# Attention's opening row maxima inside the recurrence's last steps

## The chip, the core and the metric

One NeuronCore of one Trainium2 chip runs the whole kernel in one launch. The metric is the device time of one execution in microseconds (us); less is better. The core has five engines, each with its own queue of instructions that it works through in order: PE multiplies matrices (PEld loads its weights), DVE, ACT and POOL work on vectors, and SP issues DMAs. They meet only through semaphores and, between stages, a barrier of all engines.

## The reference, cut to what matters

One decoder layer on 4096 tokens of width 1024. A projection gives the columns of three mixers; their outputs are gated, multiplied by `W_out`, normalised and added to `x`.

```python
def fox_attention(...):                        # 8 heads of 64, causal
    qh = rms_norm(heads(q), q_gain) * HEAD_DIM ** -0.5
    kh = rms_norm(heads(k), k_gain)
    cum = cumsum(log_sigmoid(f_logit + f_bias))
    s = qh @ kh.T + cum[t] - cum[s]            # s <= t
    o = softmax(s) @ vh
def rwkv7_time_mix(...):                       # 4 heads, a recurrence over all tokens
    sa = state @ -kk_t
    state = state * w_t + sa * (kk_t * a_t) + v_t * k_t
    o_t = state @ r_t                          # then group norm, gain, bias, bonus
y = concat([y_fox, y_rwkv, y_pool]) * silu(g)
x = x + gate * rms_norm(y @ w_out, norm_post)
```

## The kernel before

Five stages run one after the other, each with its own semaphores and buffers and a barrier behind it: set-up, projection (up to about 1397 us), `recur` (up to 1979.7), `attend` (up to about 3190) and `output`.

**`recur`.** The tokens are cut into 16 blocks of 256. A written-out loop, `STEPS = range(-4, BLOCKS + 1)`, runs over steps n = -4 to 16, and in step n every engine works on several blocks at once: block n+3 is prepared (gates, decays, operands), block n+2 gets its scores and its diagonal blocks inverted, block n+1 its triangular inverse, block n goes through the serial chain, block n-1 through the group norm. In steps 13 to 16 the outer blocks are gone, so what is left is the serial chain of blocks 14 and 15 and their norms. The chain of a block has two halves (chunk 0 and 1). On PE it is `right_side` (L1912, L1915), `solve` (L1923), `output` (L1943 to L1949) and `state` (L1933); between them ACT copies the results out of PSUM (`r1_out` L1719, `u_out` L1723), and DVE makes the next state, `state_passed` (L2117). The order of the calls in each engine's part of the loop is the order in its queue. At the end of the chain ACT copies the output (`o_out` L1741) and takes mean and deviation (L1657 to L1673); POOL does `bonus` (L1535, L1538) and `scaled` (L1543 to L1547, four operations on the block's output, `ost`), and SP stores the block (L1426). `negative_mean(b)` on ACT waits for the second operation of `scaled(b - 1)`. Beside all this ACT and DVE split `W_out` into two float16 parts, one row block a step: `w_high` (L1652) and `w_low` (L2135).

**`attend`.** For each of 4 turns of a hardware loop it takes two heads (slots u = 0 and 1). The scores come from two matmuls per unit of 128 keys by up to 512 queries, with the float16 operand pairs `ka`/`qa` and `kb`/`qb` (L2619, L2621). ACT takes the exponential (L2530), POOL or DVE the low part `plo` of the result (L2508, L2721), PE multiplies with `v` (L2600, L2602). The maximum of each row of scores must be known first: for each block of queries PE computes `qa x ka` once more into one of four banks `pm` (L2551 is the causal mask on the diagonal, L2552 the product), DVE takes the largest of each row (L2677). When all maxima of a block of 512 queries are there, POOL adds the decay terms (L2453), DVE takes the largest (L2693, `mp`), POOL splits it into three float16 pieces in seven small operations (L2460 to L2471, into `mw`), PE turns them (L2561) and DVE copies them as three rows of `qb` (L2685). These maxima run `AHEAD` = 49 units ahead of the scores. So before the first turn there is an opening: 49 maxima and 4 rows, 53 items on PE, numbered k = 0 to 52 here. Its operands have to be loaded first (SP, L2376 to L2392), and POOL makes two masks, two identities and constants (L2436 to L2446). Meanwhile DVE and ACT clear the upper rows of `qb` and `kb` (L2651, L2513).

## Time and profile before

| | us |
|---|---|
| runs | 3586.56, 3588.36, 3593.07 (median 3588.36) |
| profiled execution | 3581.05, its span 3579.3 |
| PE busy | 3312.7 (93%) |
| DVE busy | 2415.0 (67%) |
| ACT busy | 1970.1 (55%) |
| POOL busy | 1785.0 (50%) |
| mean granted TensorE clock | 0.96 of full |

The profile's page cuts the span in 40 slices of 89.5 us. PE is 90% busy or more in most of them. Beside the first four, the exceptions are slice 16 (4 tenths), where the recurrence begins, slices 22 and 23 (8 and 6 tenths), where the recurrence ends and attention begins, and slice 36 and the last (7 and 8), around the stage `output`. The rows of the trace that follow further on are from that stretch, from 1906 to 2019 us, but for one on the loop. A row of the timeline gives start, duration, engine, line, operation, the result's and the operands' names with their shapes, how many instructions it stands for, and in brackets how long the engine was idle before it and whom it waited for. PEclk is the granted clock of TensorE as a share of full speed: 1.00 is 2.4 GHz and 0.50 is 1.2 GHz.

### The profile page before, as it was taken

Reading aid. Unit: us, or ns where it says so; the run is one execution under the profiler, and the core shown is the slowest. Engines: PE = TensorE matmul, PEld = TensorE weight load, DVE = VectorE, ACT = ScalarE, POOL = GpSimd, SP = SyncE. Lnnn points to the kernel's source line nnn. Section 1 sums busy time; section 2 is a strip of 40 time slices with the busy share of each in tenths; the row PEclk is TensorE's granted clock in tenths of the full one; section 3 lists DMA queues with packets and bytes.
Section 4 is the critical chain, followed back from the end, with each engine's and each line's share of the span. In section 5 each row is a group of like instructions: output and inputs, shape, how many; then the busy total and the mean of one; then the engine's idle time right before and its main releaser. Section 6 shows DMA issues by size and latency. Waiting matters only on the chain. (4 is left out here: it accounts for less than half of the span.)

```text
span 3579.3 us, 90138 instructions
## 1 busy us (share of the span) xinstructions
PE 3312.7 (93%) x31944; PEld 2298.4 (64%) x31944; DVE 2415.0 (67%) x4337; ACT 1970.1 (55%) x3745; POOL 1785.0 (50%) x2083
## 2 busy tenths in 40 slices
PE   6788999999999994999998699999999999979998
PEld 6783488469549642888888366666666656644444
DVE  5787756326433335786873789899889988965554
ACT  2444544424432234676775477777777777753333
POOL 2376300510330233344553599889988889852222
PEclk9899999999999997898997899999999999989999
DMA  7387445435444533232210312021120220215555
GB/s 313 129 300 254 161 146 169 151 130 178 146 141 155 181 133 89 57 84 69 67 49 28 70 43 59 9 57 36 29 59 10 55 49 17 58 70 181 186 186 180
DMA packets 247770, 401.06 MB, mean 112 GB/s; under 512 B 85646, under 2 KB 199013, under 8 KB 232453
## 3 DMA queue, kind: packets, MB, share of 16 engines
q1 hardware_dynamic: 223979, 383.75, 33.5%
q10 hardware_dynamic: 22880, 11.54, 1.2%
q8 instruction: 258, 4.23, 0.5%
q14 instruction: 173, 1.41, 0.1%
q0 software_dynamic: 480, 0.14, 0.1%
HBM read 272.77 MB, written 122.59 MB: 110 GB/s over the span
## 5 line engine op out<-in xcount | busy, mean ns | idle before, releaser
L2530 ACT ACTIVATE p<-psc,xb,sc 128x512 f32<-128x512 f32 (+3 forms) x1152 | 848.5, 744 | 315.1 <-PE psc L2621 302.1
L2508 POOL TENSOR_TENSOR plo<-p 128x512 f16<-128x512 f32 (+2 forms) x864 | 906.8, 1078 | 66.9 <-ACT p L2530 65.8
L2677 DVE TENSOR_REDUCE mx<-pm 128x1 f32<-128x512 f32 (+3 forms) x1201 | 731.4, 636 | 99.4 <-PE pm L2552 85.8
L646 PE MATMUL bank<-h,ring 128*128 128x512 f16 x2688 | 597.8, 381 | 4.9 <-DVE u L990 4.9
L2600 PE MATMUL po<-v,p 128*128 128x129 f16 x4224 | 513.3, 220 | 20.9 <-POOL plo L2508 18.0
L651 PE MATMUL bank<-ring,h 128*128 128x128 f16 x8064 | 467.0, 222 | 26.7 <-ACT c L818 12.3
L646 PEld LDWEIGHTS bank<-h,ring 128*128 128x128 f16 x2688 | 263.9, 98 | 343.4 <-issue 42.5
L2602 PE MATMUL po<-v,plo 128*128 128x65 f16 x4224 | 483.4, 192 | 0.0
L651 PEld LDWEIGHTS bank<-ring,h 128*128 128x128 f16 x8064 | 463.6, 99 | 28.1 <-issue 12.6
L2600 PEld LDWEIGHTS po<-v,p 128*128 128x128 bf16 x4224 | 388.8, 97 | 121.3 <-POOL plo L2508 28.0
L2602 PEld LDWEIGHTS po<-v,plo 128*128 128x128 f16 x4224 | 379.2, 98 | 96.2
L2552 PE MATMUL pm<-ka,qa 128*128 128x512 f16 (+3 forms) x1201 | 436.8, 367 | 3.1 <-DVE mx L2677 3.0
L1165 POOL CAST stage<-c 128x512 f16<-128x512 f32 x64 | 47.3, 740 | 766.1 <-DVE c L1006 766.1
L2619 PE MATMUL psc<-qa,ka 128*128 128x512 f16 (+3 forms) x1152 | 419.4, 364 | 2.6 <-ACT p L2530 2.4
L2621 PE MATMUL psc<-qb,kb 128*128 128x512 f16 (+3 forms) x1152 | 417.8, 363 | 0.0
L2893 PE MATMUL pz<-wo,yh 128*128 128x512 f16 x1024 | 306.0, 381 | 3.1 <-DVE yl L2925 3.1
L1000 DVE TENSOR_TENSOR c<-bank,u 128x512 f32<-128x512 f32 x168 | 115.6, 689 | 249.6 <-PE bank L646 170.9
L2721 DVE TENSOR_TENSOR plo<-p 128x512 f16<-128x512 f32 (+1 forms) x288 | 280.1, 972 | 0.0
L2837 POOL TENSOR_TENSOR o<-o,xr 128x1024 f32<-128x1024 f32 x32 | 75.4, 2356 | 312.5 <-DVE o L2948 312.5
L2552 PEld LDWEIGHTS pm<-ka,qa 128*128 128x128 f16 x1201 | 118.4, 99 | 134.7 <-DVE mx L2677 15.6
L2893 PE MATMUL pz<-wo,yl 128*128 128x512 f16 x512 | 194.8, 380 | 0.0
L2893 PEld LDWEIGHTS pz<-wo,yh 128*128 128x128 f16 x1024 | 100.5, 98 | 117.8 <-issue 5.2
(417 smaller groups left out, 5583.3 us busy)
## 6 DMA issues: line engine op xcount, KB each, us to landing
ring<-scratch_ws SPq DMA_DIRECT2D x52, 1792.0 KB, 7.8
scratch_z<-stage SPq DMA_DIRECT2D x72, 256.0 KB, 3.2
scratch_ws<-h SPq DMA_DIRECT2D x10, 1792.0 KB, 6.7
y<-scratch_y SPq DMA_DIRECT2D x35, 512.0 KB
g<-scratch_g SPq DMA_DIRECT2D x35, 512.0 KB
xr<-in_x SPq DMA_DIRECT2D x34, 512.0 KB, 6.2
scratch_g<-stage SPq DMA_DIRECT2D x64, 256.0 KB, 6.0
scratch_qk<-stage SPq DMA_DIRECT2D x64, 256.0 KB, 2.6
```

Of the source, the lines that this page charges most:

```text
L646: t = nc.tensor.matmul(bank[b][:], m.ring[:, slot, l, bo, k, :], hh[:, side, r, ao, k, :], start=fresh and first, stop=last, skip_group_ch ...
L651: t = nc.tensor.matmul(bank[b][:, ts], hh[:, side, l, ao, k, ts], m.ring[:, slot, r, bo, k, :], start=fresh and first and tp == 0, stop=la ...
L2508: nc.gpsimd.tensor_tensor(plo[:, k % NP, 0:w], p32[:, k % NP, 0:w], hi[:, 0:w], ALU.subtract)\
L2530: nc.scalar.activation(p32[:, k % NP, 0:w], psc[k % 2][:, 0:w], ACT.Exp, bias=xb[:, u, b, x // 4:x // 4 + 1], scale=m.sc[:, 0:1]).then_inc ...
L2552: ins = nc.tensor.matmul(pm[g][:, n, 0:w], qa[:, u, j * P:(j + 1) * P], ka[:, u, q * BT:q * BT + w], start=not last, stop=True, skip_group ...
L2600: nc.tensor.matmul(o[:, oc:oc + VW], hi[:, c0:c0 + P], v[:, u, x, 0:VW], start=(x == 0 and t % 2 == 0), stop=False, skip_group_check=True)
L2602: g = nc.tensor.matmul(o[:, oc:oc + 1 + HD], plo[:, k % NP, c0:c0 + P], v[:, u, x, 0:1 + HD], start=False, stop=(x == 4 * b + t), skip_gro ...
L2619: nc.tensor.matmul(psc[k % 2][:, 0:w], ka[:, u, ks], qa[:, u, t0:t0 + w], start=not diag, stop=False, skip_group_check=diag)
L2621: nc.tensor.matmul(psc[k % 2][:, 0:w], kb[:, u, ks], qb[:, u, t0:t0 + w], start=False, stop=True, skip_group_check=diag).then_inc(qk_mm.se ...
L2677: nc.vector.tensor_reduce(mx[:, s, t, q:q + 1], pm[g][:, 0, 0:w], AX.X, ALU.max).then_inc(pm_d.sem, 1)
L2721: tt(plo[:, k % NP, 0:w], p32[:, k % NP, 0:w], hi[:, 0:w], ALU.subtract).then_inc(lo_v.sem, 1)
L2893: mm = nc.tensor.matmul(pz[u % 2][j][:], l[:, u % 2, k // 4, ks], r[:, k, j * HALF:(j + 1) * HALF], start=(k == 0 and c == 0), stop=(k == ...
```

## The change

Four things change; the loop of attention itself has the same instructions in the same order as before.

1. **Shared memory.** Some buffers of `recur` (`zf`, `zv`, `sw`, `av`, `ls`, `lc`, `ec`, `ei`, `kk`, `kfac`, `kinv`, `bt`, `kt`, `rk`, `dp`, `onesr`) and slot 0 of attention's operands become pieces of one tensor, `seam`, that lives through both stages. The operands of head 0, the masks, the maxima `mx` and the small rows lie over buffers that the recurrence needs no more after it has prepared block 15.
2. **Operands, masks and clearing move** from attention's start into steps 13 and 14 of the recurrence (`head_operands` and `head_rest` on SP, `head_masks` on POOL, `clear_rows` on DVE). What stays at attention's start is slot 1's: two DMAs, and clearing one half as much on ACT and DVE.
3. **The opening's 53 items move** into steps 15 and 16. On PE they are cut in groups 0 to 7: seven groups of four (k = 0 to 27) between the parts of the serial chain, and the last 25 (k = 28 to 52) behind it. They use two banks in turn, `bank[4 + k % 2]`, where attention had four.
4. `w_high` of the last row block goes behind `inverse_deviation(15)` on ACT.

```diff
+        GROUPS = (4, 4, 4, 4, 4, 4, 4)
# SP
+                    if n == END - 2:
+                        head_operands()
+                    if n == END - 1:
+                        sp.wait_ge(e_clear, 2)
+                        head_rest()
# POOL
+                def head_row(r):
+                    pool.wait_ge(e_done, plan.pre_end[r])
+                    row_sum(nc, m, r).then_inc(e_add, 1)
+                    pool.wait_ge(e_max, r + 1)
+                    for j in range(6):
+                        row_piece(nc, m, j, r % 2).then_inc(e_piece, 1)
+                        pool.wait_ge(e_piece, r * 6 + j + 1)
+                    row_piece(nc, m, 6, r % 2).then_inc(e_row, 1)
                     if there(n - 1):
                         bonus(n - 1)
+                    if n == END - 1:
+                        head_masks()
+                    if n == END:
+                        for r in range(3):
+                            head_row(r)
+                    if n == END + 1:
+                        for r in range(3, plan.EARLY):
+                            head_row(r)
                     ...
                     if there(n - 1):
                         scaled(n - 1)
# ACT
-                    if 0 <= n - 9 < KT:
+                    if 0 <= n - 9 < KT - 1:
                         w_high(n - 9)
                     ...
                         inverse_deviation(n - 1)
+                    if n - 9 == KT - 1:
+                        w_high(n - 9)
# PE, with END = 15; between the lines stand the calls for other blocks
+                def head_maxima(g):
+                    if g == 0:
+                        pe.wait_ge(e_first, 128)
+                        pe.wait_ge(e_made, 1)
+                    for what, item, k in opening[use_at[g]:use_at[g + 1]]:
+                        if k >= 2:
+                            pe.wait_ge(e_done, k - 1)
+                        free = bank[4 + k % 2]
+                        if what == "max":
+                            query_maximum(nc, m, free, m.qa0, m.ka0, item).then_inc(e_mm, 1)
                         right_side(n, 0)
+                        head_maxima(0)
                         solve(n, 0)
+                        head_maxima(1)
                         state(n, 0)
+                        head_maxima(2)
                         right_side(n, 1)
+                        head_maxima(3)
                         solve(n, 1)
+                        head_maxima(4)
                         output(n, 0)
                         state(n, 1)
+                        head_maxima(5)
                         output(n, 1)
+                        head_maxima(6)
+                        head_maxima(7)
# DVE
+                    if n == END:
+                        head_largest(0)
+                        head_largest(1)
                         state_passed(n, 1)
+                    if n == END:
+                        for g in range(2, 6):
+                            head_largest(g)
+                    if n == END + 1:
+                        for g in (6, 7):
+                            head_largest(g)
                     ...
+                    if n == END - 1:
+                        clear_rows()
# attention's start
-                nc.scalar.activation(kb[HD:P, :, :], m.zero[HD:P, :].unsqueeze(2).to_broadcast([HD, 2, SEQ]), ACT.Copy)\
-                    .then_inc(cleared, 1)
+                nc.scalar.activation(kb[1][HD:P, :], m.zero[HD:P, 0:1].to_broadcast([HD, SEQ]), ACT.Copy).then_inc(cleared, 1)
```

`head_largest(g)` on DVE takes the largest of each of the group's banks in turn, and the same small steps for the rows as before. Row 0 is ready for its sum after 4 items, row 1 after 13, row 2 after 26 and row 3 after 43 (`pre_end`).

PE's queue in the middle of step 15, before: `right_side` and `solve` of chunk 0 (`chain_banks<-vt,akr`, `<-Zc,ar`, `<-r,XT`), its `state` (`<-U,bkt`, `<-vt,bkt`), then `right_side` and `solve` of chunk 1.

```order
L1923 MATMUL chain_banks<-r,XT 128x64 x4
L1933 MATMUL chain_banks<-U,bkt 64x64 x2
L1933 MATMUL chain_banks<-vt,bkt 64x64 x2
L1933 MATMUL chain_banks<-U,bkt 64x64 x2
L1933 MATMUL chain_banks<-vt,bkt 64x64 x2
L1912 MATMUL chain_banks<-vt,akr 128x64 x4
L1915 MATMUL chain_banks<-Zc,ar 128x64 x4
L1923 MATMUL chain_banks<-r,XT 128x64 x4
```

PE's queue at the same place of the changed kernel, from the end of that `state` on: L1395 and L1396 are mask and product of a maximum, L2238 the turning of a row, L2179, L2182 and L2190 the chain's `right_side` and `solve`.

```order
L2200 MATMUL chain_banks<-vt,bkt 64x64 x2
L1396 MATMUL bank<-seam 128x512
L1395 MATMUL bank<-seam 128x128
L1396 MATMUL bank<-seam 128x384
L1396 MATMUL bank<-seam 128x512
L2238 MATMUL bank<-seam 128x128 x4
L2179 MATMUL chain_banks<-vt,akr 128x64 x4
L2182 MATMUL chain_banks<-Zc,ar 128x64 x4
L1395 MATMUL bank<-seam 128x128
L1396 MATMUL bank<-seam 128x512 x3
L1395 MATMUL bank<-seam 128x128
L1396 MATMUL bank<-seam 128x128
```

Group 2 now stands between `state` and `right_side`, and group 3 between `right_side` and `solve`, which comes next.

POOL's queue in steps 15 and 16, before: `scaled(14)`, `bonus(15)`, `scaled(15)`.

```order
L1543 TENSOR_TENSOR ost<-ost,st 128x512
L1544 TENSOR_TENSOR ost<-ost,st 128x512
L1545 TENSOR_TENSOR ost<-ost,lng 128x512
L1547 TENSOR_TENSOR ost<-ost,bv 128x512
L1535 TENSOR_TENSOR bv<-vt,bon 128x512
L1538 TENSOR_TENSOR bv<-bv,lnb 128x512
L1543 TENSOR_TENSOR ost<-ost,st 128x512
L1544 TENSOR_TENSOR ost<-ost,st 128x512
```

POOL's queue at the same place of the changed kernel, from the last piece of row 2 on (L1423); L1403 is the sum of row 3, L1412 to L1423 its pieces.

```order
L1423 TENSOR_TENSOR seam<-seam,fixed 128x4
L1772 TENSOR_TENSOR ost<-ost,st 128x512
L1773 TENSOR_TENSOR ost<-ost,st 128x512
L1774 TENSOR_TENSOR ost<-ost,lng 128x512
L1776 TENSOR_TENSOR ost<-ost,bv 128x512
L1764 TENSOR_TENSOR bv<-vt,bon 128x512
L1767 TENSOR_TENSOR bv<-bv,lnb 128x512
L1403 TENSOR_TENSOR seam<-seam 128x4x4
L1412 TENSOR_TENSOR seam<-seam,fixed 128x4
L1414 TENSOR_TENSOR seam<-seam,fixed 128x4
```

Rows 0, 1 and 2 now stand ahead of `scaled(14)`, and row 3 between `bonus(15)` and `scaled(15)`.

## Rows read from the trace of the kernel before

**Rows 1.** Stretches: length, busy time by engine, clock, DMA share, GB/s.

```profile
1947.00:1963.00 16.00, 15.10 (x88) 14.20 (x88) 1.32 (x2) 7.09 (x24) 3.05 (x3) 0.50 0.00 0
1963.00:1979.70 16.70, 0.00 (x0) 0.00 (x0) 1.28 (x1) 7.92 (x30) 8.47 (x8) 0.50 0.09 31
1979.70:1989.30 9.60, 0.00 (x1) 0.03 (x2) 4.18 (x4) 7.03 (x1) 3.46 (x14) 0.50 0.87 186
1989.30:2018.10 28.80, 20.28 (x82) 7.69 (x83) 27.16 (x56) 0.00 (x0) 6.58 (x32) 0.80 0.38 90
```

**Rows 2.** Timeline of PE in step 15 (start, duration, engine, line, operation).

```profile
1942.57 0.66 PE L1915 MATMUL chain_banks<-Zc,ar 64*128 64x64 f32 x8
1943.81 1.07 PE L1923 MATMUL chain_banks<-r,XT 128*128 128x64 f32 x8 [0.57 <-ACT r L1719]
...
1947.18 1.94 PE L1912 MATMUL chain_banks<-vt,akr 128*128 128x64 f32 x8 [0.72 <-DVE Zc L2117]
...
1950.75 1.94 PE L1923 MATMUL chain_banks<-r,XT 128*128 128x64 f32 x8 [0.57 <-ACT r L1719]
1952.48 1.92 PE L1943 MATMUL front<-vt,akr 128*128 128x64 f32 x8
...
1961.74 1.12 PE L1949 MATMUL front<-Zc,ar 64*128 64x64 f32 x8
```

**Rows 3.** Timeline of PE, the opening and the first score.

```profile
1989.30 0.27 PE L2551 MATMUL pm<-mq,idb 128*128 128x128 bf16 x1 [26.44 <-DMA ka<-scratch_nc]
...
2013.02 0.39 PE L2552 MATMUL pm<-ka,qa 128*128 128x512 f16 x1 [0.21 <-DVE mx L2677]
...
2016.96 0.50 PE L2561 MATMUL pm<-id,mw 128*128 128x128 f16 x4 [1.09 <-DVE mx L2677]
...
2018.11 0.31 PE L2617 MATMUL psc<-mk,idb 128*128 128x128 bf16 x1
2018.22 0.63 PE L2619 MATMUL psc<-qa,ka 128*128 128x512 f16 x1
```

**Rows 4.** Timeline of DVE, the next state and the clearing of `qb`.

```profile
1946.56 0.48 DVE L2117 SCALAR_TENSOR_TENSOR Zc<-chain_banks,facs,Zw 128x64 f32<-128x64 f32 x2 [10.25 <-PE chain_banks L1933]
...
1980.62 3.47 DVE L2651 MEMSET qb<- 64x4096 uint32 x1 [11.40 <-PEq L74]
```

**Rows 5.** Timeline of DVE, maxima in a row and one alone.

```profile
2012.28 2.48 DVE L2677 TENSOR_REDUCE mx<-pm 128x1 f32<-128x512 f32 x4
...
2017.61 0.43 DVE L2685 COPY qb<-pm 32x512 f16<-32x512 f16 x1 [0.19 <-PE pm L2561]
...
2029.17 0.68 DVE L2677 TENSOR_REDUCE mx<-pm 128x1 f32<-128x512 f32 x1
```

**Rows 6.** Timeline of POOL, steps 14 and 16 and the opening.

```profile
1937.69 1.04 POOL L1543 TENSOR_TENSOR ost<-ost,st 128x512 f32<-128x512 f32 x1 [30.72 <-ACT st L1673]
...
1971.18 1.04 POOL L1543 TENSOR_TENSOR ost<-ost,st 128x512 f32<-128x512 f32 x1 [4.08 <-ACT st L1673]
...
1974.77 1.26 POOL L1547 TENSOR_TENSOR ost<-ost,bv 128x512 f32<-128x512 f32 x1
...
2005.24 0.21 POOL L2460 TENSOR_TENSOR mw<-mp,fixed 128x4 f16<-128x4 f32 x1 [1.06 <-DVE mp L2693]
...
2006.93 0.21 POOL L2471 TENSOR_TENSOR mw<-mp,fixed 128x4 f16<-128x4 f32 x1
```

**Rows 7.** Timeline of ACT, the clearing of `kb` and the first exponential.

```profile
1979.73 7.03 ACT L2513 ACTIVATE kb<-zero 64x8192 f16<-64x8192 f32 x1 [8.69 <-PEq L74]
2019.32 0.78 ACT L2530 ACTIVATE p<-psc,xb,sc 128x512 f32<-128x512 f32 x1 [32.56 <-PE psc L2621]
```

**Rows 8.** Waits inside the attention loop: who for whom, total us, times, longest us.

```profile
PE psc L2617 <- issue: 12.1, 3, 4.2
```

**Rows 9.** Timeline of SP, the queue that issues DMAs, step 14.

```profile
1906.15 0.43 SPq L1426 DMA_DIRECT2D scratch_y<-ost  x1
1927.68 0.39 SPq L1426 DMA_DIRECT2D scratch_y<-yp  x1
```

More of the change, by code:

```diff
@@ L1351, in recur @@
         npar, nlate = 6, 11
+        plan = m.plan
+        e_first, e_second, e_clear, e_made, e_mm, e_done, e_row, e_add, e_max, e_piece = (sem("early_" + n) for n in (
+            "first", "second", "clear", "made", "mm", "done", "row", "add", "max", "piece"))
+        END = BLOCKS - 1
+        GROUPS = (4, 4, 4, 4, 4, 4, 4)
+        opening = []
+        for what, item in plan.early:
+            opening.append((what, item, sum(w != "largest" for w, i, _ in opening)))
+        use_at = [0]
+        for size in GROUPS:
+            n = use_at[-1]
+            while n < len(opening) and sum(w != "largest" for w, i, _ in opening[use_at[-1]:n]) < size:
+                n += 1
+            use_at.append(n)
+        use_at.append(len(opening))
+        OC1, OXROW = HD - 3, P - 3
         def at(l, c):
@@ L3029, in hymba_layer @@
         m.off = ctx.enter_context(nc.sbuf_tensor("off", [P, FOX_HEADS, NT], F32))
-        recur(nc, a, m)
-        attend(nc, a, m)
+        with ExitStack() as both:
+            seam(nc, both, m)
+            recur(nc, a, m)
+            attend(nc, a, m)
         output(nc, a, m)
```

518 lines of the change are left out of this document (287 added, 231 removed).

## The prediction, made before the changed kernel ran

> **What bounds the kernel now.** The page's slices show PE busy nearly everywhere except at a few seams, so I went to the seam that the diff touches, first by stretches, then by the timeline of each engine. The stretches [rows 1] show four parts. From 1947 to 1963 PE works on the serial chain of block 15. From 1963 to 1979.7 it does nothing: ACT takes the norm, POOL works off `scaled(15)`, SP stores the block, and the barrier follows. From 1979.7 to 1989.3 it does nothing again: attention's first operands are on their way (186 GB/s, DMA share 0.87; PE's first maximum waits for `ka`, 26.44 us of idle time in all [rows 3]). From 1989.3 to 2018.1 DVE is busy for 27.2 of 28.8 us with 49 maxima and 4 rows: there DVE is the bound. The first score follows at 2018.11 [rows 3], the first exponential at 2019.32 [rows 7]. So from 1979.73 [rows 7] to 2019.32 there are 39.6 us in which the attention loop has not begun, while DVE had next to nothing to do in the 32.7 us before (1.32 + 1.28 us busy, rows 1). That is what can be gained at most. The loop behind has the same instructions in the same order, so I follow one time alone, the first exponential, and move everything behind it by as much.
>
> **A maximum on two banks.** Reductions of 512 columns follow each other every 0.60 us ((2.48 - 0.68) / 3) and one takes 0.68 [rows 5]. PE starts the next product 0.06 us after a reduction (the one from 2012.28 ends at 2012.96, PE starts at 2013.02 [rows 3]) and takes 0.39; DVE starts 0.15 us after PE's end (2016.96 + 0.50 to 2017.61 [rows 3, 5]). With four banks DVE sets the pace, 0.60. With two, one bank's round is 0.06 + 0.39 + 0.15 + 0.68 = 1.28, two items in it: 0.64 an item. At TensorE's half clock a product of 512 columns takes 0.63 (2018.22 [rows 3]), and the item costs 0.76.
>
> **Groups 0 to 5 in the chain.** PE issues the first two items of a group at once, the third waits for DVE's first reduction, the fourth for the second, so a group holds PE for 1.3 to 2.2 us. Some of it lies in waits that the chain has anyway: 0.57 and 0.57 us for ACT, 0.72 for DVE [rows 2]. I walked through both queues with these durations. Before, `solve` of chunk 0 starts at 1943.81, `right_side` of chunk 1 at 1947.18, its `solve` at 1950.75, `output` of chunk 0 at 1952.48 [rows 2]. After: group 0 has narrow items (128 to 512 columns) and costs 0.8; group 1 costs 1.2; group 2 1.3, because `state_passed` (0.48 us [rows 4]) now stands behind eight reductions on DVE and ahead of the third item; group 3 1.4; group 4 2.2; group 5, with the turning of row 1, 2.0. Sum 8.8 us: `output` of chunk 1 ends at 1971.7 where it ended at 1962.86 [rows 2].
>
> **Groups 6 and 7, and POOL's queue.** The rest starts then. Row 3's sum needs the items to k = 42, 19 of them, at 0.65: 1984.1. DVE takes the largest behind two more items (1985.5), POOL's seven pieces take 1.9 (2005.24 to 2007.14 [rows 6]): 1987.5. Now the price: `scaled(15)` stands behind row 3 on POOL, and row 2, which needs an item of group 6, stands ahead of `scaled(14)`, for whose second operation ACT's mean of block 15 waits. That norm is still ready before 1987.5 (row 2 at 1976.8, two operations of `scaled(14)` 1979.0, then 6.0 us of ACT, at 1985.0), so row 3 decides. `scaled(15)` takes 4.85 us (1971.18 to 1976.03 [rows 6]): 1992.3. From its end to attention's first instruction there were 3.70 us for the store and the barrier (1976.03 to 1979.73 [rows 6, 7]): 1996.0. Before this was 1979.7: the recurrence gets 16.3 us longer.
>
> **Attention's start.** No load, no masks, no opening. But ACT still clears slot 1's rows of `kb` ahead of its first exponential. Both slots took 7.03 us [rows 7] and were hidden behind the load; one slot, 3.5 us, has no cover now. PE has its first two scores and DVE has cleared its half (1.7 of 3.47 us [rows 4]) by then. First exponential at 1999.6 instead of 2019.32: 39.6 - 16.3 - 3.5 = 19.8 us earlier.
>
> **Costed at nothing.** The operands: 2.0 MB in eight DMAs behind 1906.6 on SP, which then has nothing to issue until 1927.68 [rows 9]; before, 9.6 us moved 1.8 MB [rows 1], so they land near 1920 and PE wants them at 1943.2; if that cover were gone, every us late is one us. The masks: POOL is idle for the 30.7 us before 1937.69 [rows 6], and they are 3.5 us of work [rows 1]. `clear_rows`: its last clearing waits for PE's last transposes of step 14 and ends near 1942.9, before the first reduction. `head_rest` puts six DMAs (2.1 MB) ahead of `store(13)`; ACT needs that store's landing only to overwrite the buffer, after `output` of chunk 0, and that is now near 1964. Moving `w_high` takes 1.1 us off ACT's tail, which no longer ends last. The wait added in the loop is on DMAs long landed. The shared tensor itself moves addresses only; the trace can't price that, and I take zero.
>
> **Bounds.** The walk again with chain and items all at full clock ends the recurrence at 1989.5 (gain 26.2), with all at half clock at 2000.8 (14.9). My value has the chain at the half clock that it has now and the items at full clock, since the opening's mean of 0.80 [rows 1] is nearer to full than to half. Code for the loop: at the beginning of a later turn PE waits up to 4.2 us for nothing that shows [rows 8]; if that comes at the first turn too, the first exponential is near 5.4 us behind the barrier and not 3.5 (-1.9); nothing at all is the other end.
>
> **The sum.** 3581.05 - 19.8 = 3561.3 us for an execution like the profiled one. The median shown is 7.3 us above that execution, so I add it back: 3588.36 - 19.8 = 3568.6, say 3569.
>
> **Rival 1: the clock stays up.** Between 1947 and 1963 PE is busy for 15.1 of 16 us with a granted clock of 0.50 [rows 1], in narrow float32 products. Put wide float16 products between them and the clock may rise; each part of the chain then takes the shorter of its two durations (`solve` 1.07 instead of 1.94 [rows 2]), and with the items at full clock too the gain is 26.2: 3562. For it: in the opening, on such products, the clock was 0.80 [rows 1]. Against it: PE still waits in every group.
> The Trainium skill (TensorE: Matmul & The Clock Gate, What's actually happening) says that the clock follows how busy PE has been lately. By that rule the fuller queue speaks for 3562; the same rule would have the stretch from 1947 to 1963 at full clock already, and there the trace disagrees with it, at 0.50.
>
> **Rival 2, slower: two banks work as one.** If the hand-over costs so much that a product and a reduction never overlap, an item costs the whole round, 1.28 us, or 1.52 at half clock, not 0.64. The place is PE's wait for `e_done` in every group. Walked through: the recurrence ends at 2022.6 to 2033.8, the first exponential at 2026 to 2037, 7 to 18 us later than now: about 3601. It decides from about 1.15 us an item; at 1.0 some 10 us of gain are left (3579). Against it: PE restarts 0.06 us after a reduction, and nothing in the rows holds both banks.
>
> **Rival 3: a cold start of the loop.** Code, the uncovered clearing and half clock in the loop's first units (0.80 of the clock even now just after 2018) together give back 4 to 6 us: 3574. For it: [rows 8]; against: ACT's and POOL's first instructions followed the barrier at once.
>
> **Rival 4: it doesn't take effect.** A load or mask late enough to hold group 0 back to the end of the chain would leave the opening whole behind it: little or no gain, 3585. The 23 us of slack above speak against it.
>
> **Chances.** Forecast 0.56; rival 1 0.13; rival 2 in its full form 0.06, in the mild form (1.0 us) 0.06; rival 3 0.14; rival 4 0.05. 0.2% is 7.2 us, about what a measurement can tell here: faster is below 3581.2, same up to 3595.5. Forecast and rivals 1 and 3 are faster, of the mild form two thirds: 0.87, which I lower to 0.85 for what I don't see; same 0.09; slower 0.06. Range: 3560 (rival 1 and 2 us) to 3582 (the mild form of rival 2); the forecast's own is 3562 to 3574.
>
> **What would show it.** Attention's first instruction near 1996 and the first exponential 3.5 us behind it; `output` of chunk 1 ending near 1972; maxima 0.64 us apart in group 7; POOL doing `scaled(15)` straight behind row 3, near 1987.5, with ACT's norm done 2 us before; a turn of the loop still 293 us. Wrong it is if the maxima are 1 us apart, if PE waits for a DMA in group 0, if `scaled(15)` waits for ACT, or if the loop's turns have changed.

## The result: 3549.05 us, below the range

The changed kernel takes 3549.05 us (median of 9 executions, 3542.35 to 3574.25), the one before 3588.01 us beside it (9, 3572.18 to 3605.6). The ratio is 0.9908, 95% interval 0.9882 to 0.9934, or 24 to 42 us less. The forecast was 3569, the range 3560 to 3582. The direction and the order of events were right; the clock of the chain, and with it the size, was not.

Executions of one kernel differ here by up to 51 us, so two medians of ten runs each say little about 10 us. Over all runs of the study, on several chips, before has a mean of 3586.1 us (123 runs, standard error 1.0) and after, run three times over, 3556.1 us (28 runs, standard error 2.3): 29.9 us less. I therefore take the sizes from the traces, at places that can be laid side by side. One measure serves for all: the time from PE's first `right_side` of block 15 to the first exponential of the loop, called the seam from here on.

### The profile page after: what moved, and what is told of

It is laid out like the page before. It is cut to its first block and busy times, and to the rows that moved or that the text cites. A ratio compares the mean times of both kernels' runs of the same rounds, so it can differ in the third digit from the quotient of the medians.

```text
span 3540.6 us, 90103 instructions
## 1 busy us (share of the span) xinstructions
PE 3298.0 (93%) x31944; PEld 2282.0 (64%) x31944; DVE 2428.2 (69%) x4339; ACT 1965.7 (56%) x3745; POOL 1785.6 (50%) x2083
## 5 line engine op out<-in xcount | busy, mean ns | idle before, releaser
L2732 ACT ACTIVATE p<-psc,seam,sc 128x512 f32<-128x512 f32 (+3 forms) x1152 | 848.6, 743 | 283.1 <-PE psc L2793 270.2
L2834 DVE TENSOR_REDUCE seam<-pm 128x1 f32<-128x512 f32 (+3 forms) x1152 | 703.5, 637 | 92.4 <-PE pm L1396 80.6
L2772 PE MATMUL po<-v,p 128*128 128x129 f16 x2112 | 255.9, 220 | 11.9 <-POOL plo L2711 10.3
L2772 PE MATMUL po<-seam,p 128*128 128x129 f16 x2112 | 257.5, 220 | 9.6 <-POOL plo L2711 8.0
L2774 PE MATMUL po<-seam,plo 128*128 128x65 f16 x2112 | 242.3, 192 | 0.0
L2774 PE MATMUL po<-v,plo 128*128 128x65 f16 x2112 | 241.0, 192 | 0.0
L2772 PEld LDWEIGHTS po<-v,p 128*128 128x128 bf16 x2112 | 194.2, 97 | 63.0 <-POOL plo L2711 15.9
L2772 PEld LDWEIGHTS po<-seam,p 128*128 128x128 bf16 x2112 | 194.7, 97 | 59.4 <-POOL plo L2711 12.4
L2774 PEld LDWEIGHTS po<-seam,plo 128*128 128x128 f16 x2112 | 189.6, 98 | 49.5
L2774 PEld LDWEIGHTS po<-v,plo 128*128 128x128 f16 x2112 | 189.6, 98 | 46.8
L2791 PE MATMUL psc<-seam 128*128 128x512 f16 (+1 forms) x576 | 213.0, 370 | 0.1
L1396 PE MATMUL pm<-seam 128*128 128x512 f16 (+3 forms) x576 | 212.7, 369 | 0.0
```

The source lines that it names most:

```text
L1396: return nc.tensor.matmul(bank[:, 0:w], qa[:, j * P:(j + 1) * P], ka[:, q * BT:q * BT + w], start=not last, stop=True, skip_group_check=last)
L2732: nc.scalar.activation(p32[:, k % NP, 0:w], psc[k % 2][:, 0:w], ACT.Exp, bias=xb[:, u, b, x // 4:x // 4 + 1], scale=m.sc[:, 0:1]).then_inc ...
L2772: nc.tensor.matmul(o[:, oc:oc + VW], hi[:, c0:c0 + P], v[u][:, x, 0:VW], start=(x == 0 and t % 2 == 0), stop=False, skip_group_check=True)
L2774: g = nc.tensor.matmul(o[:, oc:oc + 1 + HD], plo[:, k % NP, c0:c0 + P], v[u][:, x, 0:1 + HD], start=False, stop=(x == 4 * b + t), skip_gro ...
L2791: nc.tensor.matmul(psc[k % 2][:, 0:w], ka[u][:, ks], qa[u][:, t0:t0 + w], start=not diag, stop=False, skip_group_check=diag)
L2834: nc.vector.tensor_reduce(mx[:, s, t, q:q + 1], pm[g][:, 0, 0:w], AX.X, ALU.max).then_inc(pm_d.sem, 1)
```

## The profile after

The profiled execution took 3542.35 us (span 3540.6). The windows of the seam, in the columns of [rows 1]:

```profile
1929.45:1951.37 21.92, 18.10 (x172) 13.34 (x171) 16.02 (x30) 10.59 (x40) 6.54 (x19) 1.00 0.43 114
1951.37:1970.60 19.23, 14.26 (x41) 3.36 (x41) 17.00 (x31) 8.01 (x30) 13.12 (x25) 0.65 0.04 14
1970.60:1976.87 6.27, 0.00 (x0) 0.00 (x0) 1.37 (x2) 0.01 (x1) 2.41 (x2) 0.50 0.12 42
1976.87:1980.50 3.63, 2.63 (x9) 1.06 (x9) 2.35 (x3) 3.61 (x1) 0.00 (x0) 0.50 0.03 7
```

The first row is the chain of block 15 with groups 0 to 5 in it: 21.92 us at a granted clock of 1.00. The second is groups 6 and 7, the third the end of `scaled(15)`, the store and the barrier, the fourth ACT's clearing of `kb`. The load (9.6 us) and the opening (28.8 us) of [rows 1] are gone. Together 51.05 us. Before, the seam was 77.78: `right_side` at 1941.54, first exponential at 2019.32 [rows 7]. That is 26.7 us less. From the first exponential to the end of the span it is 1560.0 us before and 1560.1 after, so the loop has not changed; over the other traces of this study, in which no edit touches the turns of the loop, that stretch is 1559.9 to 1565.6 us.

The two profiled executions lie 38.7 us apart. The other 12 us arose before step 15 and are not the change's: the trace of before shows half clock for 20.5 us from 1648 on, in step 6, which the diff does not touch and which takes 41.1 us there, where that of after shows none and the step takes 31.0 (the expectation of e1 puts it in steps 3 to 5).

Before's entry into block 15 and its chain; the last two rows divide the chain where its clock falls:

```profile
1930.00:1946.54 16.54, 15.41 (x168) 13.76 (x166) 3.77 (x8) 10.90 (x43) 6.94 (x6) 0.97 0.06 18
1946.54:1962.86 16.32, 15.10 (x88) 14.20 (x88) 1.76 (x3) 7.46 (x25) 2.91 (x3) 0.50 0.00 0
1941.54:1945.42 3.88, 2.83 (x28) 2.52 (x28) 0.00 (x0) 2.02 (x9) 3.33 (x3) 1.00 0.21 72
1945.42:1962.86 17.44, 16.15 (x104) 15.06 (x104) 1.76 (x3) 8.57 (x31) 2.91 (x3) 0.50 0.00 0
```

And of after, in the same columns:

```profile
1918.00:1951.37 33.37, 29.55 (x297) 23.64 (x297) 24.01 (x42) 18.34 (x67) 10.20 (x22) 1.00 0.29 75
1951.37:1958.50 7.13, 4.62 (x19) 1.39 (x19) 6.17 (x13) 0.97 (x9) 3.71 (x11) 0.92 0.00 0
1958.50:1968.84 10.34, 8.49 (x22) 1.77 (x21) 9.28 (x16) 7.03 (x22) 7.72 (x14) 0.50 0.07 25
```

Before enters block 15 at full clock and drops to the lower level 3.9 us into the chain, after two waits of PE, of 0.57 us ahead of `solve` [rows 2] and of 0.47 us ahead of `state`; the wait of 0.72 us [rows 2] comes behind the fall. After, with maxima in those waits, stays at the upper level for the whole chain and for 6 us of the items behind it. PE is no busier for it: 18.10 of 21.92 us in after's chain, 18.98 of 21.32 in before's. The wait ahead of `state` in before's timeline of PE:

```profile
1945.36 0.47 PE L1933 MATMUL chain_banks<-U,bkt 128*64 128x64 f32 x4 [0.47 <-ACT U L1723]
```

The operations of [rows 2] in after's timeline of PE, and the maxima behind the chain:

```profile
1930.49 0.66 PE L2182 MATMUL chain_banks<-Zc,ar 64*128 64x64 f32 x8
...
1932.37 1.00 PE L2190 MATMUL chain_banks<-r,XT 128*128 128x64 f32 x8
...
1937.56 1.06 PE L2179 MATMUL chain_banks<-vt,akr 128*128 128x64 f32 x8
...
1941.09 1.06 PE L2190 MATMUL chain_banks<-r,XT 128*128 128x64 f32 x8
...
1950.71 0.66 PE L2216 MATMUL front<-Zc,ar 64*128 64x64 f32 x8
...
1953.07 0.39 PE L1396 MATMUL bank<-seam 128*128 128x512 f16 x1 [0.21 <-DVE seam L2501]
1953.67 0.39 PE L1396 MATMUL bank<-seam 128*128 128x512 f16 x1 [0.21 <-DVE seam L2501]
...
1962.64 3.42 PE L1396 MATMUL bank<-seam 128*128 128x512 f16 x5
```

`right_side` and `solve` of chunk 1 take 1.06 us each, not 1.94. Maxima follow each other every 0.60 us at full clock (1953.07, 1953.67) and every 0.68 to 0.70 at half (3.42 us for five). POOL behind the chain (rows 2 and 3, `scaled(15)`):

```profile
1953.10 0.21 POOL L1403 TENSOR_TENSOR seam<-seam 128x12 f32<-128x12 f32 x1 [9.54 <-DVE seam L2501]
...
1964.14 0.21 POOL L1403 TENSOR_TENSOR seam<-seam 128x16 f32<-128x16 f32 x1 [0.65 <-DVE seam L2501]
...
1967.39 1.04 POOL L1772 TENSOR_TENSOR ost<-ost,st 128x512 f32<-128x512 f32 x1
...
1970.97 2.12 POOL L1776 TENSOR_TENSOR ost<-ost,bv 128x512 f32<-128x512 f32 x1
```

ACT, block 15's inverse deviation, the clearing and the first exponential:

```profile
1964.38 0.21 ACT L1938 ACTIVATE st<-st 128x8 f32<-128x8 f32 x1
...
1976.87 3.61 ACT L2716 ACTIVATE kb<-zero 64x4096 f16<-64x4096 f32 x1 [11.24 <-PEq L74]
1980.50 1.34 ACT L2732 ACTIVATE p<-psc,seam,sc 128x512 f32<-128x512 f32 x2
```

Row 2's sum has waited 9.54 us for an item of group 6, row 3's sum starts 12.8 us behind the chain's end, `scaled(15)` follows row 3 at once (1967.39), and ACT's inverse deviation has been there for 2.8 us (1964.59). Attention's first instruction comes 3.78 us behind `scaled(15)`, the first exponential straight behind the clearing. This is the order of events that the prediction gave. The clock was another: the chain ran at the upper level and most of what stands behind it at the lower.

## The experiments

"Chain" is the time from block 15's first `right_side` to the end of `output` of chunk 1. Times of `e1` to `e4` stand beside 34 runs of before (median 3585.02), `e5` to `e8` beside 35 (3587.88), `e9` to `e12` beside 22 (3583.05), `e13` to `e15` beside 23 (3590.58).

| run | what | chain | seam | step 14 | median (runs) | ratio to before |
|---|---|---|---|---|---|---|
| before | | 21.32 | 77.78 | 39.2 | 3588.01 (9) | |
| after | | 21.92 | 51.05 | 39.4 | 3549.05 (9) | 0.9908 |
| e1 | after again | 21.90 | 51.06 | 39.2 | 3550.16 (11) | 0.9919 |
| e11 | after again | 33.55 | 63.66 | 49.5 | 3557.72 (8) | 0.9925 |
| e2 | no group in the chain | 21.26 | 67.42 | 39.3 | 3573.19 (12) | 0.9973 |
| e3 | before, idle products in block 15 | 21.68 | 77.72 | 46.8 | 3587.16 (12) | 0.9993 |
| e8 | e3 again | 20.17 | 77.34 | 49.5 | 3587.94 (12) | 1.0019 |
| e15 | e8 and idle products in step 14 | 16.43 | 73.32 | 32.7 | 3575.88 (12) | 0.9976 |
| e4 | norm first | 33.56 | 60.17 | 49.5 | 3571.22 (12) | 0.9956 |
| e5 | e4 again | 21.91 | 51.39 | 39.3 | 3562.55 (12) | 0.9957 |
| e6 | POOL clears `kb` | 21.91 | 49.27 | 38.3 | 3567.8 (12) | 0.9939 |
| e7 | groups of six | 33.02 | 54.96 | 39.2 | 3569.29 (8) | 0.9955 |
| e12 | `w_high` back | 21.90 | 51.05 | 38.5 | 3557.79 (8) | 0.9929 |
| e9 | other order on POOL | 21.90 | 48.71 | 37.8 | 3552.94 (6) | 0.9910 |
| e10 | e9 and e6 | 21.90 | 46.79 | 39.1 | 3551.8 (9) | 0.9917 |
| e14 | e10 again | 21.90 | 46.80 | 39.3 | 3558.77 (12) | 0.9920 |
| e13 | e10 and idle products in step 14 | 21.90 | 47.16 | 33.9 | 3545.48 (6) | 0.9895 |

"Step 14" is the time between the first `right_side` of blocks 14 and 15; in the steps of the middle, where the clock stays up, it is 30 to 31 us. The half clock of step 14 does not always begin in it: 2 to 4 us behind its start in nine of these traces, but 7 to 10.5 us ahead of it in e4, e6, e8, e9, e11, e13 and e15, and 40 us ahead in e12 (so not "in step 14" in every profile, as the expectation of e13 has it). The seam depends on the instructions and the clock in it, and repeats to 0.01 us (after and e1, e10 and e14) where the clock is the same. The medians do not: e6 has after's instructions up to attention and a median almost 19 us above it.

### After again, and twice the clock of block 15 (e1, e11)

> The changed kernel once more. I measure the seam from PE's start on the chain of block 15 (right_side, chunk 0) to attention's first exponential: 77.8 us in the kernel before (1941.54 to 2019.32), 51.1 us in the changed one (1929.45 to 1980.50). Theory A (wide products between the chain's narrow ones hold TensorE's clock up): 51 us again, within 1 us, with the granted clock at full through the whole chain. Rival B (the clock happened to be up in that one execution): 52 to 58 us, since the chain at half clock costs 6 us more. The total should lie 27 us below the kernel before, not 39: the 12 us by which the changed kernel was ahead at the start of step 15 come from one spell of half clock in steps 3 to 5 of the recurrence, which the change doesn't touch, and should come and go between executions.

> After once more, on the same chip as e9, e10 and e12: to see whether the clock of block 15 and the median (3549 and 3550 twice, against 3568 for e6, which has the same instructions up to attention) are the kernel's or the executions'. If the clock is the kernel's in block 15 and chance elsewhere: the chain at full clock again, 21.9 us, first exponential at +51.0, lowest run 3542 to 3546, and a median anywhere from 3548 to 3565. If the whole clock is the kernel's: a median of 3549 to 3551 again.

e1 repeats after: ratio 0.9919 (0.9894 to 0.9944), seam 51.06. In e11 the profiled execution of the same instructions is at half clock from 8 us ahead of step 14 to the end of the seam:

```profile
1964.98:1998.53 33.55, 31.53 (x171) 23.51 (x171) 16.23 (x30) 10.29 (x38) 3.30 (x16) 0.50 0.28 74
1998.53:2018.00 19.47, 16.23 (x42) 3.65 (x41) 16.57 (x30) 8.02 (x30) 12.43 (x25) 0.50 0.04 13
```

The chain takes 33.55 us, the seam 63.66, 14.1 us less than before's and not 26.7. The prediction's two ends for this walk were 14.9 (all at half clock) and 26.2 (all at full clock). So both ends are met within 1 us, and the changed kernel has executions of both kinds. The upper end is met with some luck: it has the items behind the chain at full clock too, and in after they lost it 6 us behind the chain. The value chosen, 19.8, mixes a chain at half clock with items at full clock; no execution showed that, and after shows the reverse. The median of e11's 8 runs, 3557.72, also says that 3549 was not the kernel's for good.

### No group in the chain (e2)

> The changed kernel with all 53 items behind the serial chain (no groups between its parts); nothing else differs. Theory A: from the start of right_side to the end of output of chunk 1 it takes 21 us as in the kernel before (21.3), at half clock from a few us into it, and the seam is 21.3 + 43 items at 0.62 + 3.2 (row 3) + 4.85 (scaled) + 3.7 (store, barrier) + 3.6 (clearing) = 63 us, 15 us less than the kernel before and 12 more than the changed one. Rival B: the chain takes 15 us, at full clock, and the seam is 57 us. If the groups in the chain bring nothing at all, the seam is 51 us.

```diff
-        GROUPS = (4, 4, 4, 4, 4, 4, 4)
+        GROUPS = (0, 0, 0, 0, 0, 0, 0)
```

Seam 67.42 where 63 was expected: the chain took the 21.3 us expected, but behind it row 3's sum came after 29.8 us, not 26.7, with the clock at half, and `scaled(15)` took 5.7, not 4.85. The seam is 10.4 us shorter than before's. That is what the early loads, and an opening beside the norm, are worth alone. The other 16.4 us come from the 24 pieces of groups 0 to 5 (22 maxima and two turned rows), 0.68 us each: what an item costs behind the chain at half clock, while in the chain all 24 lengthen it by 0.66 us together (21.92 against 21.26). They are not free there: e2's chain fell to half 3.95 us in, as before's did at 3.88, and after's did not, so the groups cost time and the clock that they held gave it back. How much each is, no run splits; e15 below, at full clock with 24 products that wait for nobody, took 16.43 us, 5.5 less than after.

### Wide products in the chain without the change (e3, e8, e15)

> The kernel before, with four float16 products of 128 by 512 into the idle banks 4 and 5 at each of the six places in step 15 where the changed kernel has groups 0 to 5 (24 products that nobody reads); all the rest as before. Theory A: the clock stays at full; the products cost 0.85 us a place less the chain's waits (2.8 us in all), the chain gains 6.3 at full clock, so from right_side to the end of output of chunk 1 it takes 17.8 us instead of 21.3, and the seam 74.3 instead of 77.8. Rival B (the clock doesn't answer to such products): 27 to 29 us for the chain, seam 84 or more.

> The kernel of e3_warm once more (before, plus 24 idle float16 products of 512 columns at the places of groups 0 to 5 in block 15), whose earlier profile was at half clock from step 14 on and so said nothing. Theory (wide products between the chain's keep the clock up): chain at full clock to its end, solve 1.06 us in both chunks, chain 18 to 20 us with the products in it, first exponential at +73 to +76 (before: +77.8), 2 to 4 us faster than before. Rival (they do nothing for the clock): solve of chunk 1 at 1.94 again, chain 21 to 24, first exponential at +77 to +80.

> Before, with the idle products of e3 in block 15 and those of e13 in step 14, and nothing else of the change. Theory (clock kept up): chain of block 15 near 18 to 20 us with 24 idle products in it, step 14 at 31 to 33 us, 5 to 10 us faster than before in the median, which would be the part of the change's gain that any wide work in the waits gives. Rival (no hold on the clock): the same as before or 2 to 5 us slower, since 40 products of 0.25 us are added.

```diff
+    def warm(g):                      # step 15, at the places of groups 0 to 5
...                                    # waits for buffers
+        for j in range(4):
+            mm(bank[4 + j % 2][:, 0:512], m.woh[:, 0, 0:P], m.woh[:, 0, 0:512], start=True, stop=True)
+    def fill(places):                 # e15, e13: step 14, at those of 0, 1, 3 and 4
...                                    # waits for buffers
+        for j in range(4):
+            mm(bank[2][:, 0:512], m.woh[:, 0, 0:P], m.woh[:, 0, 0:512], start=True, stop=True)
```

The products' results are used by nothing. In the profiled executions of e3 and e8 step 14 had left the clock at half, so their seams say nothing about holding it. They show something else, the clock coming up inside the chain, 8.4 us in for e8 and 11.6 us for e3. Windows of 5 us from e8's first `right_side` on:

```profile
1958.44:1963.44 5.00, 5.00 (x24) 3.85 (x23) 0.00 (x0) 1.25 (x5) 0.00 (x0) 0.50 0.00 0
1963.44:1968.44 5.00, 5.00 (x35) 3.08 (x34) 0.48 (x2) 3.49 (x19) 0.00 (x0) 0.66 0.01 2
1968.44:1973.44 5.00, 5.00 (x43) 4.11 (x41) 1.28 (x1) 3.02 (x5) 0.00 (x0) 1.00 0.00 0
1973.44:1978.44 5.00, 5.00 (x59) 4.35 (x57) 0.00 (x0) 2.54 (x11) 1.04 (x1) 1.00 0.02 3
```

Windows of e15, whose block 15 starts at 1934.55:

```profile
1932.00:1940.00 8.00, 8.00 (x79) 6.29 (x77) 0.36 (x2) 5.22 (x24) 5.72 (x5) 1.00 0.11 36
1940.00:1948.00 8.00, 8.00 (x77) 6.28 (x76) 1.40 (x2) 5.51 (x22) 0.00 (x0) 1.00 0.01 2
```

e8 starts block 15 at 0.50, PE is filled without a gap, and 8.4 us later the clock is at the upper level and stays there to the chain's end; before's went the other way in the same place. In e15, entering at full clock, it stays: the chain takes 16.43 us with 24 products more in it than before's 21.32. Its seam is 4.5 us shorter than before's. Its step 14 is 6.5 us shorter, but that is no gain of the products alone: the half clock began 10.5 us ahead of the step, so step 13 took 34.8 us where before has 28.9, and the two steps together take 67.6 against 68.1. Its mean is 11.1 us below that of before beside it (3577.2 against 3588.3), with a ratio of 0.9976 whose interval just reaches 1 (0.9951 to 1.0000); the trace accounts for 5 of the 11 us in the stretch that the edit touches. e3 and e8, without the products in step 14, gained nothing measurable (0.9993 and 1.0019). So e15 bears out that wide products hold a clock that is up through the chain, in one trace; a gain in the whole time is likely and not shown. The theory of e3 and e8, 2 to 4 us, is too small for their runs to show, and their profiles met another clock than expected.

### The order on POOL (e4, e5, e9)

> The changed kernel with POOL's order turned: scaled(14) ahead of row 2, and scaled(15) ahead of row 3. My reading that POOL's queue sets the end: scaled(15) ends near 33.9 us after the chain's start instead of 43.6, DVE's last split of W_out ends the stage at 42.5, and the seam is 46.8 us instead of 51.1. Rival (DVE's queue of maxima ends the stage anyway): 51 us. Total against the changed kernel: 4 us less.

> The kernel of e4_norm_first once more (scaled(14) ahead of row 2, scaled(15) ahead of row 3 on POOL). Theory (TensorE's half clock in block 15 was that execution's own, not the order's doing): in this execution the chain takes 22 us again where the clock is up, attention's first instruction comes 45 to 47.5 us behind block 15's first right_side, and the median is within 10 us of after's where the mean clock is as high. Rival (the order on POOL leaves PE idle in the tail and so costs the clock): half clock all through block 15 again, the chain near 33.5, the first instruction of attention at +56, and a median near 3571 at a clock of 0.955.

> After with another order on POOL: scaled(14) ahead of row 2 (in the 9.5 us in which POOL waits for row 2's items), row 2 ahead of bonus(15), and scaled(15) ahead of row 3. Theory (in after the norm of block 15 waits for scaled(14), and scaled(15) for row 3; in e5 the same two moves gained nothing only because row 2 stood behind bonus(15) as well and held DVE for 4 us): row 2's sum at +25 to +26 behind block 15's first right_side (after: +23.7), ACT's inverse deviation at +29 (after: +34.9), scaled(15) done near +36, row 3's pieces done near +39.5, attention's first instruction at +43 to +44.5 (after: +47.4), first exponential at +47 to +48: 3 to 4 us faster than after at the same clock. Rival (row 2 still holds DVE and with it PE's last items): +47 to +48, nothing gained. At TensorE's half clock in the chain all of it 9 to 12 us later.

```
 e4, e5:  bonus(14) row 0 row 1 scaled(14) | bonus(15) row 2 scaled(15) row 3
 e9:      bonus(14) row 0 row 1 scaled(14) row 2 | bonus(15) scaled(15) row 3
 (after:  bonus(14) row 0 row 1 row 2 scaled(14) | bonus(15) row 3 scaled(15))
```

e4's profiled execution was at half clock throughout and looked like a loss (seam 60.17 where 46.8 was expected); e5, the same kernel, came out at 51.39. So the half clock was that execution's and not the order's, the first of the two theories of e5; e11 shows the same clock in after's order. At full clock the order gained nothing (51.39 against 51.05), where 0 to 2.4 us were expected. At half clock it did: e4 and e11 are alike in clock and chain (33.56 and 33.55), and e4's seam is 3.5 us shorter (60.17 against 63.66). The sums of row 2 and of row 3 in e5's timeline of POOL say why it gained nothing at full clock:

```profile
1969.60 0.21 POOL L1403 TENSOR_TENSOR seam<-seam 128x12 f32<-128x12 f32 x1
...
1980.28 0.22 POOL L1403 TENSOR_TENSOR seam<-seam 128x16 f32<-128x16 f32 x1 [3.50 <-DVE seam L2503]
```

Row 2's sum came 27.8 us behind block 15's start (after: 23.7), DVE's reduction of it stands ahead of further maxima in DVE's queue, and so row 3 came at +38.5 (after: +34.7). e9 puts row 2 ahead of `bonus(15)`: row 2 at +25.4, row 3 at +35.8, seam 48.71. 2.3 us gained where 3 to 4 were expected: row 3 is now the last on POOL, and behind its pieces PE must still turn the row and DVE copy it, 5.9 us from the last piece to attention's first instruction where `scaled(15)` needed 3.8.

### ACT's clearing of kb (e6), both (e10, e14)

> After, with slot 1's half of kb cleared by POOL at attention's start and not by ACT ahead of its first exponential (3.61 us). If that clearing alone holds the first exponential back: the first exponential comes 1.5 to 3 us earlier behind the barrier (PE's first product starts 0.7 us behind it and the exponential needs one more), so the stretch from block 15's first right_side to it is 48 to 49.5 us, not 51.1, and the time 1.5 to 3 us lower at the same clock. Rival (PE's first product is held by DVE's clearing or by code, so that the exponential moves less): below 1 us. Rival (POOL, busy until the barrier, starts late and its clearing delays the first rows of the loop): nothing gained, or the first turn longer.

> e9's order on POOL and slot 1's half of kb cleared by POOL (as in e6, which moved the first exponential from 3.6 to 1.9 us behind the barrier). If both add up: attention starts at +43 to +44.5, the first exponential at +45 to +46.5 (after: +51.1), so 5 us faster than after at the same clock, the lowest runs near 3539. Rival (they don't add, since the end is DVE's and PE's last items): first exponential at +49.

> e10 once more, beside e13 on the same chip. At full clock in block 15: chain 21.9 us, first exponential at +46.8 behind its first right_side; at half clock chain 33.6 and first exponential at +58 to +60. Median 3548 to 3556, lowest run near 3541.

```diff
-    nc.scalar.activation(kb[1][HD:P, :], m.zero[HD:P, 0:1].to_broadcast([HD, SEQ]), ACT.Copy).then_inc(cleared, 1)
+    nc.gpsimd.memset(kb[1][HD:P, :], 0.0).then_inc(kb_cleared, 1)     # on POOL
+    pool.wait_ge(kb_cleared, 1)
...                                    # SP waits for kb_cleared too
```

The clearing in e6's timeline of POOL:

```profile
1980.47 3.51 POOL L2682 MEMSET kb<- 64x4096 f16 x1 [3.77 <-POOLq L74]
```

And the first exponential in that of ACT:

```profile
1982.34 0.78 ACT L2734 ACTIVATE p<-psc,seam,sc 128x512 f32<-128x512 f32 x1 [13.10 <-PE psc L2795]
```

The first exponential comes 1.87 us behind the barrier, not 3.63: the seam is 1.8 us shorter, as expected. POOL's clearing costs nothing that a row shows: POOL's first operation of the loop comes 4.1 us behind the barrier (after: 4.6), and from the first exponential to the end of the span it is 1560.3 us (after: 1560.1). With e9's order the seam is 46.79 and 46.80 (expected 45 to 46.5): 4.25 us below after's, the sum of 2.34 and 1.78 within 0.15. In the time this is not seen: 21 runs of e10 and e14 have a mean of 3557.0 us (standard error 2.4), after's 28 one of 3556.1 (2.3).

### Groups of six (e7), w_high back (e12)

> After with groups of six, not four: 42 of the 53 pieces of the opening inside block 15's chain, 11 behind it. Theory (at full clock the items that no longer fit into the chain's waits cost the chain 0.6 us each, and the norm of block 15, 14 us behind the chain's end, then decides and not row 3): chain 29 to 31 us, attention's first instruction near +53 (after: +47.4), 5 to 6 us slower. Rival (the chain's waits still hide them): chain below 25, the first instruction at +45 to +47, up to 2 us faster. At half clock: chain near 42, first instruction near +65.

> After with the last w_high (1.13 us of ACT) back at its place of before, ahead of block 15's deviation_log. Theory (row 3 decides when scaled(15) starts, the norm is there 3 us before): ACT's inverse deviation 1.1 us later, scaled(15) straight behind row 3 as in after, first exponential at +51.0 within 0.3. Rival (the norm decides): 1.1 us later.

e7 (`GROUPS` of six) has 36 pieces in the chain, 12 more than after (not 42, as the expectation says: group 6 stands behind it). It ends at +33.02, the last 12 us of it at half clock, so later than the 29 to 31 expected, and attention starts at +51.32 (after: +47.42), 3.9 us later, 1.7 less than expected. Groups of six are slower than groups of four; how much of it is full waits and how much the clock, this trace does not split. In e12 the seam is 51.05 again: `w_high` was rightly costed at nothing.

### Idle products in step 14 (e13)

> e10 (both edits on top of after) plus 16 idle float16 products of 512 columns in step 14, four each at the places where groups 0, 1, 3 and 4 stand in step 15. In every profile so far TensorE's clock fell to half in step 14, 30 to 60 us ahead of block 15's first right_side, just after PE had waited in block 14's chain, and in two executions (e4, e11) it stayed at half through block 15. Theory (wide products in the chain's waits keep the clock up, as the groups do in step 15): no half clock in step 14 or a shorter one; the step takes 31 to 33 us, not 38 to 49; block 15 starts at full clock; 5 to 8 us faster than e14 in the median and a narrower spread. Rival (the fall comes whatever PE does there): step 14 at 39 to 41 us, 1 to 3 us slower than e14.

Step 14 of e14, which starts at 1909.79, in windows of 8 us:

```profile
1908.00:1916.00 8.00, 5.61 (x45) 5.04 (x44) 2.63 (x5) 3.37 (x11) 7.21 (x10) 0.76 0.26 49
1916.00:1924.00 8.00, 8.00 (x48) 7.68 (x48) 1.86 (x5) 3.63 (x19) 2.44 (x10) 0.50 1.00 182
1924.00:1932.00 8.00, 8.00 (x39) 6.91 (x39) 2.48 (x4) 2.27 (x7) 0.00 (x0) 0.50 0.35 83
1932.00:1940.00 8.00, 8.00 (x54) 7.56 (x54) 3.12 (x8) 2.95 (x5) 0.00 (x0) 0.75 0.11 35
```

Steps 13 and 14 of e13; step 14 starts at 1899.10. The last two rows are the half clock ahead of and behind that start:

```profile
1884.00:1892.00 8.00, 7.47 (x84) 6.66 (x80) 7.53 (x18) 4.87 (x15) 1.97 (x2) 0.94 0.17 55
1892.00:1900.00 8.00, 8.00 (x48) 7.32 (x49) 3.21 (x5) 3.98 (x18) 7.61 (x6) 0.50 0.12 16
1900.00:1908.00 8.00, 8.00 (x35) 5.93 (x35) 1.31 (x2) 0.83 (x3) 3.61 (x15) 0.50 0.94 177
1908.00:1916.00 8.00, 8.00 (x78) 6.91 (x78) 3.91 (x8) 5.40 (x23) 0.00 (x0) 0.99 0.57 122
1891.02:1899.10 8.08, 8.08 (x49) 7.28 (x48) 4.15 (x6) 3.18 (x15) 7.69 (x6) 0.50 0.09 14
1899.10:1908.09 8.99, 8.99 (x39) 6.92 (x38) 1.31 (x2) 1.62 (x6) 4.51 (x15) 0.50 0.88 163
```

In e14 the clock falls 2.3 us into the step, in a window in which PE has work for 5.61 of 8 us, and then stays at 0.50 though PE is busy without a gap, with float32 products of 64 to 256 columns; it is up again 23.9 us later. In e13 it falls as well, but 8.1 us ahead of the step and so of its first idle product, which says nothing about whether they would prevent a fall. It is up again after 17.1 us. That early rise is what the products may claim: e13 and e15, with them, are at full clock 25 and 26 us ahead of block 15, and the eleven other traces that recover before it only 13 to 14 us ahead.

Step 14 takes 33.9 us and not 39.3, but step 13 takes 32.4 and not 28.8, so the two together gain 1.8 us (66.3 against 68.1) with 16 products more; against e6 and e9, whose clock fell as early, they gain 6 (72.6 and 72.2). The time: 3545.48 (6 runs, mean 3546.3, standard error 2.4) against 3558.77 (12 runs, mean 3559.0, 3.6) for e14 on the same chip, and the widest run is 3557.0 where e14 reaches 3576. Ratio to before 0.9895 (0.9867 to 0.9924). It is the fastest kernel here, by 10 us in the mean against after's 28 runs and by 11 against the 21 of e10 and e14; six runs are few. Of the 13 us against e14 the two traces put 1.8 in the steps with the products. The rest would have to be executions in which the clock no longer stays down through block 15, or chance; one profile cannot show which.

## Why the prediction missed, step by step

- **The bound** (39.6 us from attention's first instruction to the first exponential) was right: the loop's 1560 us did not change between the two traces.
- **The step that failed** is the size of the chain's term, the 8.8 us summed up for groups 0 to 5 (its six parts add up to 8.9), and with it the choice of a chain "at the half clock that it has now". The groups made the chain 0.6 us longer, from 21.3 to 21.9, because it kept the full clock that before lost 3.9 us in. Rival 1 had it: the clock stays up, 26.2 us of gain; the traces of after, e1, e5, e6, e9, e10, e12, e13 and e14 show it, and the gain in the seam is 26.7. Of the 8.2 us that the term was too large, the rest took back 1.3: `scaled(15)` came out 0.85 longer and the items behind the chain 0.4. I gave rival 1 0.13. Against it stood only "PE still waits in every group". The row on which the forecast leaned (0.50 between 1947 and 1963 [rows 1]) is that of a chain without wide products; the opening's 0.80 [rows 1], on just these products, was the row for the kernel after.
- What holds the clock, as far as runs show: of the executions that entered block 15 at full clock, before and e2, with nothing between the chain's parts, lost it 3.9 us in, and the nine with groups of four, and e15 with idle products, kept it through the chain (e7, with groups of six, lost it for the last 12 of 33 us). e11 and e4, with groups, entered at half and stayed there; e3 and e8, with idle products of 512 columns that wait for nobody, entered at half and came up. So in these traces the groups hold a clock that is up and don't bring it back. The level at the entry is settled in steps 13 and 14, and there it varies with the same instructions; why, stays open.
- The Trainium skill (TensorE: Matmul & The Clock Gate, What's actually happening) lets the clock follow how busy PE has been. By that rule before's chain, with PE busy for 15.1 of 16.3 us, would not be at half clock; the trace has 0.50 there, and e14 has it with PE busy for 16 of 16 us. The groups do not follow it either, as the profile counts busy time: after's chain keeps full clock with PE busy for 18.1 of 21.9 us, a smaller share than before's. Busy with what seems to matter as well: e8's chain, as free of gaps as that stretch of e14, came up with products of 512 columns in it.
- **Groups 6 and 7 and POOL**: right. Row 3's sum 12.4 us behind the chain (12.8), to `scaled(15)` 3.4 (3.25), the norm ready 2.5 us before (2.8), the store and barrier 3.70 (3.78). `scaled(15)` itself took 5.7 us, not 4.85, since its last operation has 2.12 where it had 1.26 [rows 6]. Recurrence longer by 9.2 us, not 16.3.
- **The uncovered clearing of kb**: 3.5 us forecast, 3.63 measured, shown by e6 to be half avoidable.
- **Items**: 0.64 at full and 0.76 at half clock forecast; 0.60 and 0.68 to 0.70 measured. The hand-over of the two banks costs nothing. Rival 2 (1.28 us) is out.
- **Rival 3** (cold start of the loop): out; PE's first score starts 0.7 us behind attention's first instruction (1977.56 to 1976.87), and the loop behind is no longer than before's. **Rival 4**: out; group 0 waits for no load, whose last is issued at 1897.8, 33 us ahead of it.
- **Costed at nothing**: loads, masks, `clear_rows`, `head_rest`, and `w_high` (e12) cost nothing that a row shows.
- **Added up**: 3588.36 - 26.7 = 3561.7 by the seam at full clock. That is inside the range, at its low end. So of the 19.6 us between forecast and result 6.9 are the chain's clock. The other 12.7 are not in the seam: 2.3 because the base of 3588.36, three runs, lies above the mean of all 123 (3586.1), 3.2 because the difference of the means (29.9 us, standard error 2.5) is larger than the seam's, and 7.1 because the first 9 runs of after came out low: their median is 3549.05, their mean 3553.7, the mean of all 28 3556.1. The last is luck of the sample, and the 3.2, 1.3 times its standard error, may be; whether a part of it is clock kept up elsewhere stays open. The seam of e11, 14.1 us shorter and not 26.7, would make the difference smaller, not larger. The miss is not chance alone: by the difference of all runs, too, 3588.36 - 29.9 = 3558.5 lies below the range.

## What to carry to other kernels

A walk through two queues can be right within a microsecond at both levels of the clock and still miss by the choice between them: compute both, ask for each level what PE does in the waits after the change, and give them as two cases, not one in the middle. Work put into the waits of a chain of narrow products can pay for itself: here 24 pieces of 0.6 us made the chain 0.7 us longer, since they held up a clock that it lost without them; where the clock was down at the entry (e11) the chain took 12 us more. A stretch that got shorter says little alone where the stretch before it got longer, as steps 13 and 14 of e13 and e15 did. Where executions of one kernel scatter by 1%, judge an edit of a few microseconds by a stretch of the trace between two marks, and take a second profile before an order of instructions is blamed for a slow one.

## What the runs showed of the hardware

- TensorE's granted clock stayed at 0.50 for 16 us in which PE had no gap (e14, 1916 to 1932), in float32 products of 64 to 256 columns, and rose 8.4 us into block 15 in e8 and 11.6 us in e3, where float16 products of 512 columns stood between such products.
- The same instructions in step 14 took 39.4 us in one execution and 49.5 in another (after and e11), at a mean granted clock of 0.70 and 0.50. Over the executions of before the time falls by about 27 us for each 0.01 that its mean granted clock is higher (123 runs; in 34 of them 3608 us at 0.948 and 3572 at 0.962), over the 28 of after by 28.
- POOL clears 64 partitions by 4096 float16 in 3.51 us (e6), ACT in 3.61 (after); DVE, with half as many elements of 4 bytes, in 1.76 (after).
